# Softmax sums of one-tile pairs inverted on VectorE, narrow pairs turned into one PSUM bank

## The reference, cut to what matters

```python
p_sel = masked_softmax(jnp.einsum('bghtd,bgtkd->bghtk', qg, k_g), (pos <= t[:, None])[:, :, None])
o_sel = jnp.einsum('bghtk,bgtkd->btghd', p_sel.astype(v_g.dtype), v_g)
...
p_win = masked_softmax(jnp.einsum('bghtd,bkgd->bghtk', qg, k_w), wmask)
o_win = jnp.einsum('bghtk,bkgd->btghd', p_win.astype(v_w.dtype), v_w)
o = g_blk[..., 0:1] * o_cmp + g_blk[..., 1:2] * o_sel + g_blk[..., 2:3] * o_win
```

## Time and profile before

| what | before |
|---|---|
| median of 3 runs | 1748.3 us (1747.49 to 1748.5) |
| the profiled execution | 1748.23 us |
| its span, from the first to the last instruction | 1746.4 us |
| mean granted TensorE clock | 0.995 of full speed |
| busy share: TensorE, weight loads, VectorE, ScalarE, GpSimd | 98%, 87%, 56%, 47%, 55% |
| largest parts of the chain that ended last | TensorE 86%, VectorE 8%, issue 3%, ScalarE 2%, GpSimd 1% |
| inversions on GpSimd (L2898) | 64, 702 ns each |

### The profile page before, as it was taken

How to read it: one execution, slowest core, us unless ns; L and a number is a source line. 1 busy time by engine, 2 the same in 40 slices (tenths; PEclk the granted TensorE clock), 3 DMA queues, 4 the chain that set the end, 5 groups by cost and what they waited for, 6 DMA issues and landing times.

```text
span 1746.4 us, 27720 instructions
## 1 busy us (share of the span) xinstructions
PE 1712.6 (98%) x10482; PEld 1522.1 (87%) x10482; DVE 970.9 (56%) x1638; ACT 825.4 (47%) x1667; POOL 966.7 (55%) x703
## 2 busy tenths in 40 slices
PE   8999999999999999999999999999999999999998
PEld 6988887888888998999888978888988889989996
DVE  4345664244438871586058469984333498428832
ACT  4224553232335552455256358874533556426642
POOL 4544332235444874677446459982842468638862
PEclk9999999999999999999999999999999999999999
DMA  6422122123351433233435330012531223323331
GB/s 226 119 76 60 49 73 58 49 61 98 113 169 49 121 115 115 73 97 116 127 91 148 97 107 3 6 33 73 169 109 61 77 69 107 124 73 109 110 121 48
DMA packets 222902, 161.57 MB, mean 93 GB/s; under 512 B 9769, under 2 KB 197425, under 8 KB 222770
## 3 DMA queue, kind: packets, MB, share of 16 engines
q1 hardware_dynamic: 221712, 158.73, 30.4%
q10 hardware_dynamic: 1058, 1.07, 0.2%
HBM read 155.57 MB, written 2.11 MB: 90 GB/s over the span
## 4 chain that ended last, share of the span: by engine, by line
PE 86%; DVE 8%; issue 3%; ACT 2%; POOL 1%; DMA 0%; DVEq 0%; SPq 0%; ACTq 0%
PE psum L365 26%; PE psum L367 26%; PE psum L366 26%; DVE nprobL L2871 2%; DVE stat L2864 1%; PE psum L1172 1%; PE psum L451 1%; PE psum L2785 1%; DVE ffn_quarters L2071 1%; PE psum L1183 1%; DVE ffn_tl L2081 1%; PE psum L1195 1%; PE psum L1249 1%; PE psum L1231 0%; DVE oT L2882 0%
## 5 line engine op out<-in xcount | busy, mean ns | idle before, releaser
L352 POOL TENSOR_TENSOR w_low<-ring,w_high 128x1024 fp32r<-128x1024 f32 (+2 forms) x223 | 488.7, 2202 | 537.5 <-ACT w_high L344 537.1
L365 PE MATMUL psum<-hT,w_high 128*128 128x256 f32 (+1 forms) x1120 | 380.8, 340 | 0.0
L367 PE MATMUL psum<-hT,w_low 128*128 128x256 f32 (+1 forms) x1120 | 375.2, 335 | 0.0
L366 PE MATMUL psum<-hL,w_high 128*128 128x256 f32 (+1 forms) x1120 | 375.2, 335 | 0.0
L344 ACT ACTIVATE w_high<-ring 128x1024 fp32r<-128x1024 f32 (+2 forms) x223 | 211.3, 953 | 298.6 <-PE psum L367 288.4
L367 PEld LDWEIGHTS psum<-hT,w_low 128*128 128x128 f32 x1120 | 212.6, 190 | 22.0
L365 PEld LDWEIGHTS psum<-hT,w_high 128*128 128x128 f32 x1120 | 212.9, 190 | 19.5 <-DVE hL L470 0.2
L366 PEld LDWEIGHTS psum<-hL,w_high 128*128 128x128 f32 x1120 | 212.9, 190 | 19.1
L1840 POOL TENSOR_TENSOR w_low<-ffn_sums,w_high 128x512 fp32r<-128x512 f32 x120 | 164.1, 1381 | 75.0 <-ACT w_high L1835 74.9
L1840 POOL TENSOR_TENSOR w_low<-ring,w_high 128x512 fp32r<-128x512 f32 x120 | 164.6, 1383 | 47.5 <-ACT w_high L1835 46.0
L365 PE MATMUL psum<-ffn_th,w_high 128*128 128x256 f32 x640 | 182.4, 285 | 5.5 <-POOL w_low L1840 2.8
(11 more groups left out here) (447 smaller groups left out, 3723.4 us busy)
## 6 DMA issues: line engine op xcount, KB each, us to landing
ring<-in_w_in SPq DMA_DIRECT2D x58, 512.0 KB, 3.6
ring<-in_ffn_w_up SPq DMA_DIRECT2D x44, 512.0 KB, 3.8
ring<-in_w_gate SPq DMA_DIRECT2D x22, 512.0 KB, 3.8
ring<-in_w_up SPq DMA_DIRECT2D x22, 512.0 KB, 4.8
ring<-in_w_down SPq DMA_DIRECT2D x20, 512.0 KB, 4.0
ring<-in_ffn_w_down SPq DMA_DIRECT2D x20, 512.0 KB, 3.8
ring<-in_nsa_w_in SPq DMA_DIRECT2D x18, 512.0 KB, 3.6
ring<-in_ca_wkv SPq DMA_DIRECT2D x16, 512.0 KB, 3.7
```

The costliest lines, as they stand in the source:

```text
L352: nc.gpsimd.tensor_tensor(tile_view(w_low, n, SPLIT), tile_view(ring, n, RING), tile_view(w_high, n, SPLIT), ALU.subtract).then_inc(w_lo, 1)
L365: nc.tensor.matmul(ps, lhsT=sh, rhs=mh, start=first, stop=False)
L366: nc.tensor.matmul(ps, lhsT=sh, rhs=ml_, start=False, stop=False)
L367: return nc.tensor.matmul(ps, lhsT=sl, rhs=mh, start=False, stop=last)
```

## The change

It does three things in the stage of the pairs.

- For the 16 pairs of one key tile the sums are inverted by VectorE's reciprocal in place of GpSimd's power of -1. VectorE does it for pair s-1 at step s, between the peak of pair s and the low part of pair s-3. A second counter, `p_inverted_v`, tells of it, and `wait_inverted` picks the counter by the pair. GpSimd keeps the inversion of the other 48 pairs, with one more wait, on its own earlier scaling.
- Pairs of one or two key tiles (`in_one`) have both heads turned into one bank, 4 or 5 by the pair's parity, in place of one bank for each head. turn() signals once for both heads.
- For those 32 pairs ScalarE makes the high part of both heads in one instruction and VectorE the low part of both in one. turn() waits for the low parts of the pair two before; where the width changes between narrow and wide, for both low parts of the pair just before.

```diff
+        def wait_inverted(eng, p):
+            narrow = npairs[p][1] == 0
+            eng.wait_ge(p_inverted_v if narrow else p_inverted, sum((npairs[i][1] == 0) == narrow for i in range(p + 1)))
...
+        def in_one(p):
+            return npairs[p][1] <= 1
+        def turned_to(v_):
+            p, wd = v_ // 2, (npairs[v_ // 2][1] + 1) * P
+            return bank[4 + p % 2][:, v_ % 2 * wd:v_ % 2 * wd + wd] if in_one(p) else bank[4 + v_ % 2][:, 0:wd]
+        def turned_heads(p):
+            wd = (npairs[p][1] + 1) * P
+            at_ = 2 * (p % 2)
+            if in_one(p):
+                return [(2 * p + 1, bank[4 + p % 2][:, 0:2 * wd].rearrange("p (h c) -> p h c", c=wd), slice(at_, at_ + 2), wd)]
+            return [(v_, turned_to(v_), v_ % 4, wd) for v_ in (2 * p, 2 * p + 1)]
...  turn, on TensorE
-                    if v_ >= 2:
+                    if p >= 1 and in_one(p) != in_one(p - 1):
+                        pe.wait_ge(p_low, 2 * p)
+                    elif p >= 2 and in_one(p):
+                        pe.wait_ge(p_low, 2 * p - 2)
+                    elif p >= 1:
                         pe.wait_ge(p_low, v_ - 1)
...
-                    mm.then_inc(p_turned, 1)
+                    if not in_one(p):
+                        mm.then_inc(p_turned, 1)
+                if in_one(p):
+                    mm.then_inc(p_turned, 2)
...  ScalarE
-                for v_ in ((2 * s - 6, 2 * s - 5) if s >= 3 else ()):
+                for v_, src, at_, wd in turned_heads(s - 3) if s >= 3 else ():
                     a.wait_ge(p_turned, v_ + 1)
-                    nc.scalar.activation(nprobT[:, v_ % 4, 0:(t + 1) * P], bank[4 + v_ % 2][:, 0:(t + 1) * P],
-                                         ACT.Copy).then_inc(p_high, 1)
+                    nc.scalar.activation(nprobT[:, at_, 0:wd], src, ACT.Copy).then_inc(p_high, 2 if in_one(s - 3) else 1)
...
-                            a.wait_ge(p_inverted, s - 2)
+                            wait_inverted(a, s - 3)
...  VectorE
+                if 1 <= s <= n_np and npairs[s - 1][1] == 0:
+                    p = s - 1
+                    v.wait_ge(p_exped, 2 * p + 2)
+                    if p >= 2:
+                        v.wait_ge(p_scaled, 2 * p - 2)
+                    nc.vector.reciprocal(np_recip[p % 2], np_total[p % 3]).then_inc(p_inverted_v, 1)
+                for v_, src, at_, wd in turned_heads(s - 3) if 3 <= s < n_np + 3 else ():
                     v.wait_ge(p_high, v_ + 1)
-                    nc.vector.tensor_tensor(nprobL[:, v_ % 4, 0:(t + 1) * P], bank[4 + v_ % 2][:, 0:(t + 1) * P],
-                                            nprobT[:, v_ % 4, 0:(t + 1) * P], ALU.subtract).then_inc(p_low, 1)
+                    nc.vector.tensor_tensor(nprobL[:, at_, 0:wd], src, nprobT[:, at_, 0:wd],
+                                            ALU.subtract).then_inc(p_low, 2 if in_one(s - 3) else 1)
...  GpSimd
+                if i == 0 and t > 0:
+                    g_.wait_ge(p_exped, v_ + 2)
+                    g_.wait_ge(p_scaled, max(2 * p - 2, 0))
+                    nc.gpsimd.tensor_tensor(np_recip[p % 2], np_total[p % 3], minus_one, ALU.pow).then_inc(p_inverted, 1)
                 if i == 0:
-                    g_.wait_ge(p_exped, v_ + 2)
-                    nc.gpsimd.tensor_tensor(np_recip[p % 2], np_total[p % 3], minus_one, ALU.pow).then_inc(p_inverted, 1)
-                    g_.wait_ge(p_inverted, p + 1)
+                    wait_inverted(g_, p)
```

More of the change, by code:

```diff
@@ L2746, in build @@
         np_recip = [stat[:, 30 + 2 * i:32 + 2 * i] for i in range(2)]
+        p_inverted_v = sem("np_inverted_v", nsa)
+        def wait_inverted(eng, p):
+            narrow = npairs[p][1] == 0
+            eng.wait_ge(p_inverted_v if narrow else p_inverted, sum((npairs[i][1] == 0) == narrow for i in range(p + 1)))
         def unit_of(v_):
@@ L2781, in turn @@
                     pe.wait_ge(p_scaled, v_ + 1)
-                    if v_ >= 2:
+                    if p >= 1 and in_one(p) != in_one(p - 1):
[3 more added lines that the diff above has]
+                    elif p >= 1:
                         pe.wait_ge(p_low, v_ - 1)
+                    to = turned_to(v_)
                     for j in range(t + 1):
-                        mm = nc.tensor.transpose(bank[4 + v_ % 2][:, j * P:(j + 1) * P], nprob[:, v_ % 8, j * P:(j + 1) * P], ident)
-                    mm.then_inc(p_turned, 1)
+                        mm = nc.tensor.transpose(to[:, j * P:(j + 1) * P], nprob[:, v_ % 8, j * P:(j + 1) * P], ident)
+                    if not in_one(p):
+                        mm.then_inc(p_turned, 1)
+                if in_one(p):
+                    mm.then_inc(p_turned, 2)
             def values(p):
@@ L2828, in _ @@
             for s in range(n_np + 3):
-                for v_ in ((2 * s - 6, 2 * s - 5) if s >= 3 else ()):
-                    t = npairs[v_ // 2][1]
+                for v_, src, at_, wd in turned_heads(s - 3) if s >= 3 else ():
                     a.wait_ge(p_turned, v_ + 1)
-                    if v_ >= 4:
-                        a.wait_ge(p_summed, v_ // 2 - 1)
-                    nc.scalar.activation(nprobT[:, v_ % 4, 0:(t + 1) * P], bank[4 + v_ % 2][:, 0:(t + 1) * P],
-                                         ACT.Copy).then_inc(p_high, 1)
+                    if s >= 5:
+                        a.wait_ge(p_summed, s - 4)
+                    nc.scalar.activation(nprobT[:, at_, 0:wd], src, ACT.Copy).then_inc(p_high, 2 if in_one(s - 3) else 1)
                 if s < n_np:
@@ L2865, in _ @@
                                             ALU.max, negate=True).then_inc(p_peaked, 1)
-                for v_ in ((2 * s - 6, 2 * s - 5) if 3 <= s < n_np + 3 else ()):
-                    t = npairs[v_ // 2][1]
+                if 1 <= s <= n_np and npairs[s - 1][1] == 0:
[5 more added lines that the diff above has]
+                for v_, src, at_, wd in turned_heads(s - 3) if 3 <= s < n_np + 3 else ():
                     v.wait_ge(p_high, v_ + 1)
-                    if v_ >= 4:
-                        v.wait_ge(p_summed, v_ // 2 - 1)
-                    nc.vector.tensor_tensor(nprobL[:, v_ % 4, 0:(t + 1) * P], bank[4 + v_ % 2][:, 0:(t + 1) * P],
-                                            nprobT[:, v_ % 4, 0:(t + 1) * P], ALU.subtract).then_inc(p_low, 1)
+                    if s >= 5:
+                        v.wait_ge(p_summed, s - 4)
+                    nc.vector.tensor_tensor(nprobL[:, at_, 0:wd], src, nprobT[:, at_, 0:wd],
+                                            ALU.subtract).then_inc(p_low, 2 if in_one(s - 3) else 1)
                 if s >= 6 and s % 2 == 0:
```

## The result

The changed kernel took 1755.26 us (median of 6 runs, 1753.07 to 1758.08), the kernel before on the same chip 1748.4 us (6 runs, 1747.32 to 1749.61): 1.0042 times as long, 95% interval 1.0031 to 1.0052. The forecast was 1748.8 us with 1751.1 as its upper end, so it was 6.5 us too low. The profiled execution took 1754.36 us, its span is 1752.6 us against 1746.4.

A forecast was written before the change was run, and what follows sets the result against it. TensorE, busy 98% of the span, was taken as the bound, with TensorE, VectorE and GpSimd limiting different stretches of the pair stage. Group 0 (-0.55, about +0.1) plus 3 x 0.35 gave +0.6: 1748.23 to 1748.8 us, range 1745.7 to 1751.1.

The forecast's parts named there:

- Whatever shortens the pair stage moves the end by as much: Whole kernel: TensorE only multiplies behind the pair stage, so a gain there moves the end equally; only that stage changes.
- The start, group 0: First 16 pairs: GpSimd's earlier first scaling and fewer later waits give -0.55 us; two-tile pairs cost about +0.1.
- The reciprocal, +0.155 a group: VectorE's fourth reciprocal, for pair 19, lies on the chain: +0.155 us a group, bounds 0 and 0.25.
- The change of width: Where narrow and wide pairs meet, both heads wait for both low parts: 0, at most one head's transposes.
- The banks of the narrow pairs: Group 1: pair 17 -0.06, pairs 19 and 20 +0.05 each, 21 +0.04, 23 +0.11; 18 and 22 give their gains back.
- GpSimd's queue from pair 20 on: Groups 1 to 3: if this queue set the pace, removing 12.8 us would shift its start, making the costing at nothing wrong.
- My costing of the 12.8 us at nothing in groups 1 to 3: 16 inversions leaving GpSimd save it 12.8 us, worth 0 in groups 1 to 3, where TensorE limits the one-tile pairs.
- Rival 3: Peak-exponential-copy-low ring closes on every narrow pair: 1.38 us a group, 5.5 in all, less 0.55: 1753.2 us; chance 0.10.

The follow-up runs named there:

- one_bank_only: The kernel before with only the shared banks and single copies and subtractions for one- and two-tile pairs, GpSimd inverting all pairs: 1751.51 us, ratio 1.0017.
- a_gentle: a_order with turn() at a change of width waiting only for the subtraction that frees the bank it writes: 1748.41 us, ratio 1.0010.
- a_order: The changed kernel with GpSimd's split at the cross-attention output norm waiting for VectorE's first scaling: 1750.55 us, ratio 1.0019.
- b_shift: The kernel before with 98 one-element memsets added in VectorE's idle time, its pair stage untouched: 1752.25 us against 1747.03, ratio 1.0031.

## Why the prediction was wrong

- **"Whatever shortens the pair stage moves the end by as much, because behind it TensorE only multiplies; and the change touches this stage alone."** This step failed, and it cost 3.9 of the 6.1 us. Behind the stage TensorE also waits: there is a norm where VectorE and GpSimd, both released by ScalarE, were 0.06 us apart. The change took thirty rows (instructions and waits) from VectorE's list and put one instruction at a place where 0.2 us pass. I had looked at no stage but the one that was edited. The same race is run at three more norms of the kernel before, where VectorE's second scaling leads the split by 0.05 to 0.06 us as well (at 523.08, 876.65 and 1215.01). With the order set there, the time is 1750.55 us, inside the forecast's range; but the stage itself is longer by 1.7 to 2.1 us (148.15 to 148.62 against 146.49), not by 0.6, for the reasons below.
- **The start, group 0: -0.55 for the inversions, +0.1 for the banks.** The inversions gave -0.46 to -0.79 in the three runs with no two-tile pair banked (32.71 to 33.04 against 33.50), and TensorE took over as next late. The term for the banks was mis-sized: with the two-tile pairs banked most or all of the gain is gone, whatever the waits (33.30 to 33.74 in six traces). one_bank_only shows the whole loss, 0.74.
- **The reciprocal, +0.155 a group.** Right in place, +0.05 to +0.10 in size: the bound of 0 "if it overlaps like its neighbours" was the nearer one.
- **The change of width, "0, at most one head's transposes".** This term failed: 0.27 a group (35.61 against 35.34). Head 0 of pair 16 had waited for head 0 of pair 15 alone; now it waited for both, and TensorE stood 0.27 us where by my own reading it was the limit (10.00 of 10 us busy), so nothing gave the time back. The change back to wide, at pair 24, delays that turn alone.
- **The banks of the narrow pairs.** One tile: the terms cancelled in the forecast, and they do (35.05 against 35.05). Two tiles: I had +0.05, +0.04 and +0.11, together 0.20 (with 22's gain given back), and it is 0.30. For pair 23 I counted the longer copy alone, less slack; that both heads must be turned first, and the longer step from ScalarE to VectorE, add 0.20 more, and what I gave pairs 20 and 21 doesn't come on top.
- **GpSimd's queue from pair 20 on**, which I named as a possible mistake, appears in the chain, up to the turn of pair 23 at 1087.05. It hands a delay on and makes none: measured from turn(13), its last scaling of pair 23 ends 0.22 us later than before in the changed kernel, where TensorE's stand at pair 16 makes the exponentials late, but 0.06 us earlier in a_gentle, where that stand is gone and the queue is in the chain as well. My costing of the 12.8 us at nothing in groups 1 to 3 stands.
- **Rival 3** (the ring closes on every narrow pair, 5.5 us less the start) had the right kind of cause, the wait for ScalarE's whole copy, but it closes at pair 23, not at all eight: 0.62 a group and not 1.38. That the time came near its 1753.2 is chance.

Taken one by one for a group: 0.07 for the reciprocal, 0 for one-tile banks, 0.30 for two-tile banks, 0.27 for the waits at the width: 0.64, measured 0.62, forecast 0.35. The terms don't simply add, though: one_bank_only has 0.62 without the reciprocal.

## What to carry to other kernels

Fusing two small instructions saves little where they ran back to back (0.07 us here) and costs the overlap of the heads with the engines ahead and behind (0.40 us at pair 23); before fusing, follow one item through turn, copy and subtraction and see which engine waits. A change of an engine's instruction count moves everything behind it in its list, so an unchanged stage can lose more than the edited one gains: match the two traces instruction by instruction to the end before explaining a difference by the edit. Where two engines contend and stand hundredths of a microsecond apart, put the order into the program; one semaphore wait took 3.7 us out of (d). A wait that is made coarser costs most on the engine that is the limit at that moment, so ask of each wait in which stretch it falls.

## What the runs showed of the hardware

- VectorE's scaling of 128x512 with two SBUF inputs took 0.74 us ahead of GpSimd's two-input split and 2.84 us behind it; the split itself 2.94 and 2.42 us. The one that began second waited for the first: in both kernels' traces such a scaling ended 0.54 to 0.55 us behind the split.
- At one place in VectorE's list an instruction started 0.2 us late, in both traces of the changed kernel and in a_order, and in b_shift at the same place (0.32 us) and again 128 places on (0.23 us). The kernel before has no such delay at these two places; what decides it is open.
- A stand of 2 us of TensorE was followed by 3.4 us at the lower clock (0.50 over 1384.7 to 1388.1); where TensorE did not stand there, the clock stayed at 1.00.
